# Early modulation pieces by one feature chunk with scale and shift together, their totals through a turned PSUM bank and a matmul with a constant matrix

## The reference

```python
cond = jax.nn.silu(c)                                  # (1, 1024)
mod = cond @ w_ada[l] + b_ada[l]                       # (1, 9 * 1024)
sh1, sc1, gt1, sh2, sc2, gt2, sh3, sc3, gt3 = split(mod, 9)
u = rms_norm(h, g_ffn1[l]) * (1.0 + sc1) + sh1         # (512, 1024)
h = h + 0.5 * gt1 * swiglu(u, w_ffn1_in[l], w_ffn1_out[l])
...
```

## Time and profile before

| | us |
|---|---|
| median of 3 runs (lowest to highest) | 1189.61 (1189.26 to 1191.75) |
| the profiled execution: its own time | 1190.7 |
| its span in the trace | 1189.0 |
| TensorE busy, share of the span | 1171.0, 98% |
| VectorE busy, share of the span | 908.4, 76% |
| ScalarE busy, share of the span | 609.2, 51% |
| TensorE share of the chain of work that ended last | 89% |

### The profile page before, as it was taken

The page is one execution under the profiler, slowest core; times in us unless marked ns, Lnnn a source line. Parts: engine busy times, 40 slices in busy tenths (PEclk is TensorE's granted clock), DMA queues, the critical chain, the costliest instruction groups (busy, mean ns, idle before and its releaser), DMA issues.

```text
span 1189.0 us, 21269 instructions
## 1 busy us (share of the span) xinstructions
PE 1171.0 (98%) x7975; PEld 1007.1 (85%) x7975; DVE 908.4 (76%) x1396; ACT 609.2 (51%) x960; POOL 59.5 (5%) x98
## 2 busy tenths in 40 slices
PE   7999999999999999999999999999999999999998
PEld 5789999888888887777787878788889999998887
DVE  5679999798886793788586657579799999988552
ACT  5646666332222675766773435444546666654331
POOL 1000000001110000000402110003000000000000
PEclk9999999999999999999999999999999999999999
DMA  9663333798773233222233222864233333342440
GB/s 327 190 165 108 101 104 106 233 294 269 238 231 97 71 106 89 54 59 67 54 97 100 67 71 79 248 190 146 71 106 107 106 106 106 106 134 75 112 115 27
DMA packets 235062, 152.62 MB, mean 128 GB/s; under 512 B 8021, under 2 KB 216046, under 8 KB 234990
## 3 DMA queue, kind: packets, MB, share of 16 engines
q1 hardware_dynamic: 230890, 149.62, 43.0%
q10 hardware_dynamic: 4100, 2.02, 0.6%
HBM read 145.31 MB, written 6.29 MB: 128 GB/s over the span
## 4 chain that ended last, share of the span: by engine, by line
PE 89%; DVE 4%; ACT 3%; DMA 1%; issue 1%; SPq 0%; ACTq 0%; DVEq 0%
PE tail L2354 8%; PE tail L2358 7%; PE tail L2363 7%; PE region L2445 7%; PE region L2449 7%; PE region L2442 7%; PE tail L2344 5%; PE tail L2346 5%; PE tail L2345 5%; PE region L2354 3%; PE region L2358 3%; PE region L2363 3%; PE tail L2442 2%; PE tail L2449 2%; PE tail L2445 2%; PE region L2344 2%
## 5 line engine op out<-in xcount | busy, mean ns | idle before, releaser
L872 ACT ACTIVATE w_hi<-raw 128x1024 fp32r<-128x1024 f32 (+1 forms) x147 | 165.1, 1123 | 246.0 <-PE tail L2363 142.6
L1458 DVE TENSOR_TENSOR w_lo<-raw,w_hi 128x1024 fp32r<-128x1024 f32 (+1 forms) x144 | 188.6, 1310 | 60.3 <-ACT w_hi L872 60.0
L2344 PE MATMUL tail<-u_hi,w_hi 128*128 128x512 f32 x264 | 107.8, 408 | 1.8 <-DVE w_lo L1458 0.9
L2346 PE MATMUL tail<-u_hi,w_lo 128*128 128x512 f32 x264 | 103.1, 391 | 0.0
L2345 PE MATMUL tail<-u_lo,w_hi 128*128 128x512 f32 x264 | 103.0, 390 | 0.0
L1666 DVE TENSOR_TENSOR w_lo<-raw,w_hi 128x512 fp32r<-128x512 f32 (+1 forms) x124 | 86.7, 699 | 14.5 <-ACT w_hi L944 10.0
L1468 DVE SCALAR_TENSOR_TENSOR ada_acc<-ada_raw,cond,ada_acc 128x512 f32<-128x512 f32 x98 | 73.5, 750 | 3.9
L944 ACT ACTIVATE w_hi<-raw 128x512 fp32r<-128x512 f32 x92 | 58.0, 631 | 15.5 <-DVE raw L1683 9.7
L948 ACT ACTIVATE work<-region 128x256 f32<-128x256 f32 x106 | 40.2, 379 | 49.0 <-PE region L2449 28.9
L2354 PE MATMUL tail<-g_hi,w_hi 128*128 128x512 f32 x264 | 64.3, 391 | 0.0
L2358 PE MATMUL tail<-g_lo,w_hi 128*128 128x512 f32 x264 | 64.1, 390 | 0.0
(11 more groups left out here) (525 smaller groups left out, 2700.6 us busy)
## 6 DMA issues: line engine op xcount, KB each, us to landing
raw<-in_w_ffn_in SPq DMA_DIRECT2D x168, 256.0 KB, 3.2
ada_raw<-in_w_ada SPq DMA_DIRECT2D x56, 512.0 KB, 5.0
raw<-in_w_in SPq DMA_DIRECT2D x90, 256.0 KB, 3.3
raw<-in_w_ffn_out SPq DMA_DIRECT2D x32, 384.0 KB, 4.5
raw<-in_w_ffn_out SPq DMA_DIRECT2D x32, 320.0 KB, 3.6
ada_early<-in_w_ada SPq DMA_DIRECT2D x8, 1024.0 KB, 10.8
gates<-kept_gates SPq DMA_DIRECT2D x16, 256.0 KB, 3.0
raw<-in_w_out SPq DMA_DIRECT2D x16, 256.0 KB, 3.3
```

What stands on the lines that cost most here:

```text
L872: act.activation(w_hi[:, slot % 2, 0:k, :], raw[:, slot, 0:k, :], ACT.Copy).then_inc(hi_ready, 1)
L1458: dve.tensor_tensor(w_lo[:, slot % 2, 0:k, :], raw[:, slot, 0:k, :], w_hi[:, slot % 2, 0:k, :].bitcast(f32), ALU.subtract).then_inc(lo_rea ...
L2344: pe.matmul(bank(b), wh, xh, start=start and n == 0, stop=False)
L2346: ins = pe.matmul(bank(b), wl, xh, start=False, stop=stop and n == k - 1)
```

## The change

A piece now holds 128 columns of the scale and the same 128 columns of the shift, so piece `a` is all that chunk `a` needs. It comes in two DMAs of 512 KiB, whose runs are 512 bytes long where they were 1024. The PSUM bank is no longer copied by ScalarE: VectorE turns it block by block (32 x 32) into `turned_parts` (`early_turn`), and TensorE multiplies the constant matrix `same_row` (1 where two partitions have the same number modulo 32) with eight of its columns. The result has each total in a 32-partition strip, and VectorE adds the bias strip by strip, in four instructions for scale and shift together. Every engine now goes through the prologue chunk by chunk and no longer by pairs.

```diff
@@ -28,7 +28,7 @@
 EPS = 1e-6
 MODS = 9
 PIECE = 256
-EARLY = 2 * D // PIECE
+EARLY = D // P
 LATE = 2 * KD
 RAW = 4
 ROUNDS = (MODS * KD - LATE) // 4
@@ -320,8 +315,8 @@
             vec_rows = sb("vec_rows", [96, P], stack=s)
             c_rows = sb("c_rows", [KD, P], stack=s)
             x_nat = sb("x_nat", [P, NB, D], stack=s)
-            ada_early = sb("ada_early", [P, EARLY, KD, PIECE], stack=s)
-            parts = sb("parts", [P, 2, PIECE], stack=s)
+            ada_early = sb("ada_early", [P, EARLY, 2, KD, P], stack=s)
+            turned_parts = sb("turned_parts", [P, 2, PIECE], stack=s)
             x_sq = sb("x_sq", [P, D], stack=s)
         with ExitStack() as s:
             g_hi, g_lo = sb("g_hi", [P, KF, S], f32r, stack=s), sb("g_lo", [P, KF, S], f32r, stack=s)
@@ -671,9 +666,11 @@
             for b in range(NB):
                 sp.dma_start(x_nat[:, b, :], x[0, b * P:(b + 1) * P, :]).then_inc(x_in[b], 16)
             for a in range(EARLY):
-                sp.dma_start(ada_early[:, a], w_ada_v[:, :, early_col(a):early_col(a) + PIECE]).then_inc(ada_early_in[a], 16)
-                if a % 2:
-                    for k in (a - 1, a):
+                for row in (1, 0):
+                    sp.dma_start(ada_early[:, a, row], w_ada_v[:, :, row * D + a * P:row * D + (a + 1) * P])\
+                        .then_inc(ada_early_in[a], 16)
+                if a % 2 == 0:
+                    for k in (a, a + 1):
                         for half in range(2):
                             sp.dma_start(raw_tiles[:, FIRST * k + 2 * half:FIRST * k + 2 * half + 2, :],
                                          ffn_in_v[0][:, k, half * FF:half * FF + 2 * P].rearrange("p (t n) -> p t n", n=P))\
@@ -1065,13 +1062,6 @@
             act.wait_ge(vec_ps, 2)
             act.activation(vec[:, :], bank(5)[:, 0:96], ACT.Copy).then_inc(vec_ready, 1)
 
-            def early_part(a):
-
-                act.wait_ge(early_ps, a + 1)
-                if a >= 2:
-                    act.wait_ge(early_cols, a - 1)
-                act.activation(parts[:, a % 2, :], bank(6 + a % 2)[:, 0:PIECE], ACT.Copy).then_inc(early_copied, 1)
-
             def first_hi(k):
 
                 act.wait_ge(first_in[k // 2], 64)
@@ -1080,26 +1070,16 @@
                 act.activation(wh_tiles[:, first_tile(k):first_tile(k) + FIRST, :],
                                raw_tiles[:, FIRST * k:FIRST * k + FIRST, :], ACT.Copy).then_inc(hi_ready, 1)
 
-            early_part(0)
             act.wait_ge(tok_ps, 1)
             act.activation(rstd[:, :], bank(4), ACT.Copy).then_inc(rstd_ready, 1)
-            early_part(1)
-            for k in range(0, KD, 2):
+            for k in range(KD):
                 first_hi(k)
-                first_hi(k + 1)
-                act.wait_ge(early_mod, k + 2)
-                for k1 in (k, k + 1):
-                    act.wait_ge(normed_ready, k1 + 1)
-                    act.activation(u_hi[:, k1, :], work[:, k1 % 2, :], ACT.Identity,
-                                   bias=mod[:, SH[0] * KD + k1:SH[0] * KD + k1 + 1]).then_inc(u_hi_ready, 1)
-                if k + 2 < KD:
-                    early_part(k + 2)
-                for k1 in (k, k + 1):
-                    act.activation(full[0][:, k1, :], work[:, k1 % 2, :], ACT.Identity,
-                                   bias=mod[:, SH[0] * KD + k1:SH[0] * KD + k1 + 1]).then_inc(t_step, 1)
-                if k + 2 < KD:
-                    early_part(k + 3)
-                if k == 2:
+                act.wait_ge(early_mod, k + 1)
+                act.wait_ge(normed_ready, k + 1)
+                shift = mod[:, SH[0] * KD + k:SH[0] * KD + k + 1]
+                act.activation(u_hi[:, k, :], work[:, k % 2, :], ACT.Identity, bias=shift).then_inc(u_hi_ready, 1)
+                act.activation(full[0][:, k, :], work[:, k % 2, :], ACT.Identity, bias=shift).then_inc(t_step, 1)
+                if k == 3:
                     act.preload_act_table_set("silu_and_others")
                     act.activation(mean_64r[:, :], mean_64[:, :], ACT.Copy)
             act.wait_ge(t_step, FULL_STEPS[0])
@@ -1966,11 +1946,22 @@
             copy_x(2 * NB - 2)
             copy_x(2 * NB - 1)
 
+            def early_turn(a):
+
+                dve.wait_ge(early_ps, a + 1)
+                if a >= 2:
+                    dve.wait_ge(early_cols, a - 1)
+                dve.transpose(turned_parts[:, a % 2, :], bank(6 + a % 2)[:, 0:PIECE]).then_inc(early_copied, 1)
+
             def early_columns(a):
 
-                cols = slice(early_col(a) // P, early_col(a) // P + 2)
                 dve.wait_ge(early_cols, a + 1)
-                dve.tensor_tensor(mod[:, cols], bank(5 - a % 2)[:, cols], vec[:, cols], ALU.add).then_inc(early_mod, 1)
+                totals = bank(5 - a % 2)[:, 0:8].rearrange("p (m t) -> p m t", t=4)
+                both, biases = (t[:, 0:2 * KD].rearrange("p (m k) -> p m k", k=KD)[:, :, a] for t in (mod, vec))
+                for t in range(4):
+                    own = slice(P // 4 * t, P // 4 * t + P // 4)
+                    ins = dve.tensor_tensor(both[own], totals[own, :, t], biases[own], ALU.add)
+                ins.then_inc(early_mod, 1)
 
             def first_lo(k):
 
@@ -1983,28 +1974,23 @@
 
                 early_columns(a)
                 dve.wait_ge(early_mod, a + 1)
-                ks = slice(a, a + 2)
-                ins = dve.scalar_tensor_tensor(scale_col[:, 0, ks], mod[:, KD + a:KD + a + 2], 1.0,
-                                               vec[:, 72 + a:74 + a], ALU.add, ALU.mult)
-                ins.then_inc(early_scale, 1)
-                dve.wait_ge(early_scale, a // 2 + 1)
-
+                dve.scalar_tensor_tensor(scale_col[:, 0, a:a + 1], mod[:, KD + a:KD + a + 1], 1.0,
+                                         vec[:, 72 + a:73 + a], ALU.add, ALU.mult).then_inc(early_scale, 1)
+                dve.wait_ge(early_scale, a + 1)
+
+            early_turn(0)
             dve.wait_ge(vec_ready, 2)
             dve.wait_ge(rstd_ready, 1)
-            for k in range(0, KD, 2):
+            for k in range(KD):
                 first_scale(k)
-                if k:
+                if k >= 2:
                     dve.wait_ge(t_step, k - 1)
                 scaled(0, k, rstd[:, :])
-                early_columns(k + 1)
                 first_lo(k)
                 low(0, k)
-                if k:
-                    dve.wait_ge(t_step, k)
-                scaled(0, k + 1, rstd[:, :])
-                first_lo(k + 1)
-                low(0, k + 1)
-                dve.wait_ge(u_lo_ready, k + 2)
+                if k + 1 < KD:
+                    early_turn(k + 1)
+            dve.wait_ge(u_lo_ready, KD)
             ffn_in(0, F1_IN)
             ada_rows(OUT_PIECE // 4 - 1)
             ada_mods(0)
@@ -2536,13 +2522,13 @@
             pe.transpose(bank(5)[:, 0:96], vec_rows[:, :], ident[0:96, 0:96]).then_inc(vec_ps, 1)
             def early_piece(a):
 
-                pe.wait_ge(ada_early_in[a], 16)
+                pe.wait_ge(ada_early_in[a], 32)
                 if a >= 2:
                     pe.wait_ge(early_copied, a - 1)
                 for k in range(KD):
                     t = k % 4
                     ins = pe.matmul(bank(6 + a % 2)[32 * t:32 * t + 32, 0:PIECE],
-                                    cond[:, k:k + 1].to_broadcast([P, 32]), ada_early[:, a, k, :],
+                                    cond[:, k:k + 1].to_broadcast([P, 32]), ada_early[:, a, :, k, :],
                                     start=k < 4, stop=k >= 4, tile_position=(0, 32 * t))
                 ins.then_inc(early_ps, 1)
 
@@ -2550,16 +2536,14 @@
 
                 pe.wait_ge(early_copied, a + 1)
                 if a == 0:
+                    pe.wait_ge(masks, 13)
                     pe.wait_ge(vec_ready, 2)
                 if a == 1:
                     pe.wait_ge(rstd_ready, 1)
                 if a >= 2:
                     pe.wait_ge(early_mod, a - 1)
-                for n in range(2):
-                    col = early_col(a) // P + n
-                    ins = pe.matmul(bank(5 - a % 2)[:, col:col + 1], parts[:, a % 2, n * P:(n + 1) * P], share[:, 0:1],
-                                    start=True, stop=True)
-                ins.then_inc(early_cols, 1)
+                columns = turned_parts[:, a % 2, :].rearrange("p (c j) -> p c j", j=P // 4)[:, :, 0]
+                pe.matmul(bank(5 - a % 2)[:, 0:8], same_row[:, :], columns, start=True, stop=True).then_inc(early_cols, 1)
 
             def first_half(k, j):
 
@@ -2588,24 +2572,19 @@
                                    ident[:, :])
             ins.then_inc(tok_ps, 1)
             early_totals(0)
-            early_piece(1)
-            early_totals(1)
             pe.wait_ge(h_ready, KD)
             pe.matmul(bank(0), ident[:, :], x_nat[:, 0, 0:S], start=True, stop=True)
+            early_piece(1)
             for k in range(KD):
                 ins = first_half(k, 0)
```

(18 more changed lines are left out.)

## The result

The changed kernel takes 1193.06 us (median of 10 runs, 1192.35 to 1193.72), the kernel before 1190.02 on the same chip (10 runs, 1189.26 to 1191.99): ratio 1.0023, 95% interval 1.0014 to 1.0031, so 1.7 to 3.7 us slower. The forecast was 1190.0, within 1188.4 to 1192.3. The profiled execution of the changed kernel took 1193.19 us by its own time.

What follows compares the result with a forecast made beforehand. TensorE was taken as the bound, with the DMA queue full beside it. Terms of -0.07, -1.24, +1.51 and +0.18 summed to +0.38 us, a median of 1190.0 us, range 1188.4 to 1192.3.

Steps and rivals of the forecast that it cites:

- Term 1: Start of chunk 0: piece 1 lands at 17.18 with the queue at 307 GB/s, chunk 0 starts at 18.18, -0.07 us.
- Rival B: Piece loads: 512-byte runs are as fast as long ones, chunk 0 starts at 17.36, 1189.2 us; chance 0.15.
- Term 2: Chunks 0 to 5: cheaper totals matmuls, TensorE binds at 4.30 us a chunk, the chain just inside at 4.25; -1.24 us.
- rival C: Prologue chunks: four additions make the chain 4.5 us, above TensorE's 4.30, and bind each chunk; 1191.4 us, chance 0.13.
- Term 3: Chunk 6: only its second half covers the chain, so it takes 4.25 us, +1.51, about 0.9 of it TensorE waiting.
- Term 4: From chunk 7 into the main loop: first matmul 3.60 us after chunk 7 starts, against 3.42 before; +0.18 us.
- The worst case of my bounds: Whole forecast: queue at 289 GB/s, no saving on totals, additions of 0.16 us each; +2.3 us.
- Rival D: Piece loads: sustained short runs make the queue the bound, below 278 GB/s by piece 7; 1195.3 us at 250, chance 0.10.
- Rival F: Main loop: it swallows the shift from the prologue, leaving 1189.6 us; chance 0.04.

Runs made afterwards that it cites:

- the third run: The changed kernel with totals from four narrow matmuls, so that VectorE needs one addition instead of four; 1195.35 us, ratio 1.0042.
- the first run: The changed kernel with the identity product ahead of piece 1 run three times, to keep TensorE busy; 1193.08 us, ratio 1.0019.
- the last: The kernel before with its pieces in runs of 512 bytes and extra identity products keeping TensorE busy; 1194.14 us, ratio 1.0029.

## Why the prediction failed

**Term 1 failed, at the rate of the queue.** I took 307 GB/s from a stretch of 4 us because it was the longest; the pieces came at 290 in every kernel with short runs, and the low end of that same stretch was 289. At 290 two pieces take 7.23 us and not 6.83, which is 0.40 of the 0.58 us by which piece 1 came later than I had it (17.76, not 17.18). A chunk's loads, a piece and half a weight group, take 4.37 us (1.311 MB at 300 GB/s, the mean of 30.0 to 42.0) and not 4.17: more than TensorE's own 4.16 and just under the 4.40 at which the chunks followed each other, so that no slack was left. The rest of the term's miss, 0.87 us of 1.45, I didn't foresee at all: TensorE, idle for 2.06 us on this landing, did piece 1 at the half clock. The Trainium skill (DMA: Bandwidth & Descriptors, Specifications) has 512 bytes as enough for line rate; this case differs, 290 against 349 GB/s, and the measurement decides. Rival B falls with it.

**Term 2 had the right chain and priced it from the wrong row.** Six chunks took 26.99 us where I had 25.83 (27.07 - 1.24). Chunk 0 took 5.00 for the half clock; the five others 4.40, because the four additions bind, which was rival C. The totals got cheaper than I had it, and TensorE's own work is 4.16 us and not 4.30, but the chain is longer. From the first addition to the scaling it is now 0.90 us (48.41 to 49.31); I had 0.39 and 0.24 for three more additions, and each of the three took 0.17, not 0.08. I wrote that nothing in the trace has four such in a row. That was a misreading: the kernel before adds the biases of its later modulations in the same way, far behind the prologue.

```profile
270.70 1.38 DVE L1514 TENSOR_TENSOR mod<-region,vec 32x8 f32<-32x8 f32 x8
...
367.18 0.68 DVE L1514 TENSOR_TENSOR mod<-region,vec 32x8 f32<-32x8 f32 x4
```

Four additions on 32 partitions take 0.68 us there, 0.17 each. With that my chain would have been 4.52 us, above my 4.30 for TensorE, and C the forecast. The Trainium skill (VectorE: DVE Perf Modes, the section on the TRN2 errata) names a fixed extra latency for each instruction that reads from SBUF, as these do with the bias. The rows agree: 0.17 us whether an addition has two elements or eight. What the additions cost by themselves no run shows, since the third run also lengthened TensorE's work; it can't be much, with the queue's 4.37 us just beneath their 4.40.

**Term 3 was right**, a chunk 6 that waits for its chain: 4.40 us for 4.25, with 1.16 us of waiting for 0.9; the additions took 0.27 more than I had and the rest of the chain 0.12 less. **Term 4 was right**, 3.67 for 3.60.

Added up, the forecast's +0.38 and the misses, 1.45 (Term 1), 1.16 and 0.15 (Terms 2 and 3) and 0.07 (Term 4), are the 3.21 us that were measured. The worst case of my bounds, +2.3, had the rate and the additions in it but not the clock, which stands at 0.87 us in piece 1 and 0.60 in chunk 0. But the runs show that these are places and not causes that add: with the clock at full chunk 0 gained 0.53 us and chunk 1 1.10, and the wait for piece 3 left 0.35 of it at chunk 2. In the changed kernel itself TensorE waits for the queue only up to piece 1; behind it the additions set the pace, and the queue was the bound just beneath. Rival D's mechanism shows where the clock is taken out (the first run and the last), but not where I had put it: piece 7 came in time (45.38), and at 290 GB/s, not below 278, the queue already set pieces 1 and, in the first run, 3. My sum let pieces queue up ahead of TensorE with 0.13 us to spare in each chunk; no slack was left for a landing 0.6 us late at the start. Rival F is excluded, since the main loop passed on all of it.

**What the change could have had otherwise** isn't settled by removing its faults: with long runs, one addition, full clock and the totals early, the main loop is still 1.87 us late (53.35), since chunk order with paired pieces holds chunk 0 to 20.24. No version here beats the kernel before. Long runs and one chunk's data together would need another layout of the weights in memory, and weren't tried.

## What to carry to other kernels

Where a queue and an engine are within a few per cent of each other, price the queue at the lowest rate that the trace shows for the run length, not at a mean with a burst in it, and set it against the engine chunk by chunk. A row that gives the distance behind one operation doesn't price four in a row: look for the same operation in the whole trace, also far behind the stage in question, and where there is none, count each at its own duration. When one wait is removed, look in the trace for the wait behind it before booking the gain.

## What the runs showed of the hardware

Runs of 512 bytes held 290 GB/s for as long as only pieces were under way, 1024-byte runs 348 to 349, in the same queue and stretch; one run took 34 and 51 ns (medians), so that half the length took two thirds of the time. TensorE's granted clock fell in six of the seven profiles without added products, after stretches in which it had waited for the queue (2.06 us in the changed kernel, 0.75 in the kernel before, there in one of two executions). In all five others, with two to four products whose result nobody reads, it stayed at 1.00 there, at no gain in the median (0.9998 in the kernel before). Four additions on 32 partitions follow each other 0.17 us apart on VectorE, with two elements each or with eight.
